# A layer's down-projection as seven half products instead of eight

## The reference, cut to what matters

```python
def conv_mlp(h, w_up, conv_w, w_down):
    u = dwconv3(h @ w_up, conv_w)
    gate, val = jnp.split(u, 2, axis=-1)
    return (jax.nn.silu(gate) * val) @ w_down      # (1024, 2816) @ (2816, 1024)

x = x + rmsnorm(y, norm_ffn_post)                  # y: the result of conv_mlp
h = rms_norm(x, l0_norm_2)                         # then the second block's first products
```

## Time and profile before

| | |
|---|---|
| Median of three runs | 1764.63 us (1763.34 to 1764.92) |
| Span of the profiled execution (the page gives no other time of it) | 1762.3 us |
| PE busy | 1737.1 us, 99% of the span |
| DVE, ACT, POOL busy | 1205.0, 787.1, 468.5 us |
| Down stage | 870.7 to 1111.4 us from the span's start |
| Mean granted TensorE clock | 0.999 |

### The profile page before, as it was taken

The page is one execution under the profiler, slowest core; times in us unless marked ns, Lnnn a source line. Parts: engine busy times, 40 slices in busy tenths (PEclk is TensorE's granted clock), DMA queues, the critical chain, the costliest instruction groups (busy, mean ns, idle before and its releaser), DMA issues.

```text
span 1762.3 us, 21154 instructions
## 1 busy us (share of the span) xinstructions
PE 1737.1 (99%) x8280; PEld 1424.6 (81%) x8280; DVE 1205.0 (68%) x1331; ACT 787.1 (45%) x1015; POOL 468.5 (27%) x201
## 2 busy tenths in 40 slices
PE   8999999999999999999999999999999999999998
PEld 5778888888787788888888888877888888888787
DVE  6454677859898887887764676755576767676534
ACT  5332222245335554544442443423366666666622
POOL 3357555364000000000164345122321211201151
PEclk9999999999999999999999999999999999999999
DMA  5233222145311222222464355412310111102232
GB/s 183 108 108 109 83 84 84 37 133 176 122 72 40 104 82 74 96 72 84 143 216 148 116 194 176 155 48 72 107 55 27 34 49 36 48 12 84 78 131 96
DMA packets 60588, 170.80 MB, mean 97 GB/s; under 512 B 7760, under 2 KB 10192, under 8 KB 60496
## 3 DMA queue, kind: packets, MB, share of 16 engines
q1 hardware_dynamic: 43216, 122.24, 20.9%
q10 hardware_dynamic: 17280, 47.30, 7.1%
HBM read 131.24 MB, written 38.27 MB: 96 GB/s over the span
## 4 chain that ended last, share of the span: by engine, by line
PE 89%; DVE 5%; ACT 3%; DMA 1%; issue 1%; ACTq 0%; SPq 0%; DVEq 0%
PE psum L732 21%; PE psum L1037 16%; PE psum L1050 14%; PE psum L771 5%; PE psum L1176 5%; PE psum L1201 5%; PE psum L927 5%; PE psum L1103 4%; PE psum L1210 4%; PE psum L1190 3%; DVE ptl L2492 2%; PE psum L753 1%; ACT pth L1824 1%; PE psum L1128 1%; PE psum L1310 1%
## 5 line engine op out<-in xcount | busy, mean ns | idle before, releaser
L643 POOL TENSOR_TENSOR wl<-wstage,wh 128x1024 fp32r<-128x1024 f32 x90 | 229.9, 2557 | 224.5 <-ACT wh L1337 192.2
L638 POOL TENSOR_TENSOR wh<-wstage,ones 128x1024 fp32r<-128x1024 f32 x43 | 103.0, 2396 | 463.3 <-PE psum L1176 298.8
L643 POOL TENSOR_TENSOR wx<-wstage,wx 128x1024 fp32r<-128x1024 f32 x25 | 61.5, 2462 | 493.6 <-ACT wx L1337 493.6
L732 PE MATMUL psum<-hh,wh 128*128 128x512 f32 x544 | 174.4, 402 | 0.0
L732 PE MATMUL psum<-hl,wh 128*128 128x512 f32 x544 | 168.0, 390 | 0.0
L732 PE MATMUL psum<-hh,wl 128*128 128x512 f32 x544 | 167.7, 389 | 0.0
L2213 DVE SCALAR_TENSOR_TENSOR cc<-uu,col,cc 128x1023 f32<-128x1023 f32 x88 | 114.9, 1306 | 44.6 <-ACT cc L1553 43.0
L732 PEld LDWEIGHTS psum<-hh,wh 128*128 128x128 f32 x544 | 100.2, 188 | 26.5 <-issue 5.6
L732 PEld LDWEIGHTS psum<-hh,wl 128*128 128x128 f32 x544 | 102.1, 188 | 21.9
L732 PEld LDWEIGHTS psum<-hl,wh 128*128 128x128 f32 x544 | 102.1, 188 | 21.6
L2492 DVE TENSOR_TENSOR ptl<-psum,pth 128x1024 fp32r<-128x1024 f32 x64 | 78.3, 1224 | 58.0 <-ACT pth L1824 58.0
(11 more groups left out here) (388 smaller groups left out, 4465.9 us busy)
## 6 DMA issues: line engine op xcount, KB each, us to landing
wstage<-w_units SPq DMA_DIRECT2D x161, 512.0 KB, 3.8
acts<-cc ACTq DMA_DIRECT2D x22, 512.0 KB, 2.6
hhf<-acts SPq DMA_DIRECT2D x27, 256.0 KB, 4.0
mix<-spill ACTq DMA_DIRECT2D x12, 512.0 KB, 2.6
resid<-yo SPq DMA_DIRECT2D x24, 256.0 KB, 2.2
hlf<-acts SPq DMA_DIRECT2D x17, 256.0 KB, 4.1
kq<-mix SPq DMA_DIRECT2D x16, 256.0 KB, 3.9
rstd<-gates ACTq DMA_DIRECT2D x16, 256.0 KB, 2.9
```

Of the source, the lines that this page charges most:

```text
L638: pool.tensor_tensor(high, stage(u), ones[:, :].unsqueeze(1).to_broadcast([P, 8, P]), ALU.mult).then_inc(w_high, 1)
L643: pool.tensor_tensor(low, stage(u), high.bitcast(F32), ALU.subtract).then_inc(w_split, 1)
L732: mm = pe.matmul(out[:, t], w[:, wslot, b, :], x[part][:, xk, t], start=start and n == 0, stop=stop and n == 2)
```

## The change

The stage is cut into blocks: the weights into W11, W21 (tiles 0 to 10, output tiles 0 to 3 and 4 to 7) and W12, W22 (tiles 11 to 21), the activations by tiles 0 to 10 and 11 to 21 and by T0 and T1. Instead of eight products of half size seven are made (f = 0 to 6), of `DK` = 11 steps each, with four output tiles a step: 12 matmuls a step, 77 steps. Several products need sums of weight blocks or of activation blocks as operands; DVE makes them in the stage (`left_sum`, `half_sums`), from blocks loaded half by half (`load_left`, `load_block`, `load_right`). POOL makes the low part of each weight half unit and the last product's activation difference. Two products that share a term share a PSUM bank: it is copied out by ACT (`taken`) and then goes on accumulating, and DVE adds the later ones to `yo` (`joined`).

| f | left (weights) | sum by DVE | right (activations) | sum | result to |
|---|---|---|---|---|---|
| 0 | W11 | none | tiles 0-10, T1 | none | m 0-3, T1 |
| 1 | W21 + W22 | yes | difference of T0 and T1 | DVE | m 4-7, T0 |
| 2 | f1's minus W11 | yes | tiles 11-21, T0 minus f1's | DVE | m 0-3, T0 |
| 3 | W12 minus f2's | yes | tiles 11-21, T0 | none | added, m 0-3, T0 |
| 4 | W11 minus W21 | yes | difference | DVE | added, m 4-7, T0; copied, T1 |
| 5 | W12 | none | tiles 11-21, T1 | none | added, m 0-3, T1 |
| 6 | W22 | none | difference | POOL | m 4-7, T1 |

The core of the diff:

```diff
+DK = FT // 2
+DOWNS = 7 * DK
 # PE
-            for half in range(2):
-                for k in range(FT):
-                    pe.wait_ge(w_split, U_DOWN + half * FT + k + 1)
-                    pe.wait_ge(a_lo, half * FT + k + 1)
...
+            def down(s):
+                f, p = divmod(s, DK)
+                high, low = left_place(s)
+                pe.wait_ge(w_split, U_DOWN + s + 1)
+                pe.wait_ge(a_lo, s + 1)
+                for m in range(4):
+                    if p == 0:
+                        down_free(f, m)
                     for n, (w, x) in enumerate(((high, ah), (high, al), (low, ah))):
...
+            for s in range(DOWNS):
+                down(s)
+                if s == 5 * DK + 3:
+                    pe.wait_ge(y_odd, 8)
+                    pe.wait_ge(y_even, 13)
+                    sum_half(0, KT - 1, 3)
 # places: weights in a ring of 4 half units, activations in one of 5
+            if U_DOWN <= u < U_L0:
+                return u - 3
 # SP
+            load_right(0)
+            load_right(1)
+            for s in range(DOWNS):
+                load_left(s)
+                if s + 2 < DK:
+                    load_right(s + 2)
+                if s < DK:
+                    load_block(s)
+                if 5 <= s < 5 + 2 * DK:
+                    load_right(DK + s - 5)
+                if 3 * DK + 5 <= s < 4 * DK + 5:
+                    load_block(DK + s - 3 * DK - 5)
+                if 4 * DK + 5 <= s < 5 * DK + 5:
+                    load_right(3 * DK + s - 4 * DK - 5)
 # POOL
+            def left_low(s):
+                pool.wait_ge(w_act, BY_ACT.index(U_DOWN + s) + 1)
+                high, low = left_place(s)
+                pool.tensor_tensor(low, left_source(s), high.bitcast(F32), ALU.subtract).then_inc(w_split, 1)
+            def last_right_sum(p):
+                pool.wait_ge(a_lo, 5 * DK + p + 1)
+                pool.tensor_tensor(right_z[p], right_z[p], right_x[p], ALU.subtract).then_inc(last_right, 1)
+            for s in range(DOWNS):
+                left_low(s)
+                if 5 * DK + 4 <= s < 6 * DK + 4:
+                    last_right_sum(s - 5 * DK - 4)
 # ACT
+            def down_parts(s):
+                right_half_high(s)
+                left_high(s)
+            def residual_moved(k):
+                residual_tile(2, 0, k, C_L0)
+                act.dma_start(resid2[k, :, T0], yo[:, k, T0]).then_inc(res_out, DMA)
+                if k + 2 < KT:
+                    act.dma_start(xr[:, k % 2, T0], resid1[k + 2, :, T0]).then_inc(xr_in[k % 2][0], DMA)
+            for s in range(7, DOWNS):
+                down_parts(s)
...
+                if s == 5 * DK + 6:
+                    half_roots(0, KT - 1, 3)
+                if 5 * DK + 7 <= s < 5 * DK + 7 + KT:
+                    residual_moved(s - 5 * DK - 7)
 # DVE
+            def half_sums(s):
+                f, p = divmod(s, DK)
+                if 1 <= f <= 4:
+                    left_sum(s)
+                if f in (1, 2):
+                    dve.wait_ge(*right_loaded(f * DK + p))
+                    dve.tensor_tensor(right_x[p], (right_z, right_w)[f - 1][p], right_x[p], ALU.subtract).then_inc(sw_sum, 1)
+                elif f == 4:
+                    dve.tensor_tensor(right_w[p], right_w[p], right_z[p], ALU.subtract).then_inc(sw_sum, 1)
+            def a_low(s):
+                half_sums(s + 2)
+                dve.wait_ge(a_hi, s + 1)
+                dve.tensor_tensor(al[s % DEEP], right_source(s), f32(ah[s % DEEP]), ALU.subtract).then_inc(a_lo, 1)
+            for s in range(7, DOWNS):
+                a_low(s)
...
+                if s == 5 * DK + 6:
+                    half_inverse(0, 3)
+                if 5 * DK + 7 <= s < 5 * DK + 7 + KT:
+                    residual_tile(2, 0, s - 5 * DK - 7, C_FPOST, C_L0)
```

More of the change, by code:

```diff
@@ L42 @@
 U_DOWN = U_SW + 7 * NS
-U_L0 = U_DOWN + 2 * FT
+DK = FT // 2
+DOWNS = 7 * DK
+U_L0 = U_DOWN + DOWNS
 U_ATT = U_L0 + 14
@@ L594, in _ @@
                 load_pair(q)
[L595 to L600, removed]
+            load_right(0)
[12 more added lines that the diff above has]
+                    load_right(3 * DK + s - 4 * DK - 5)
+            load(U_L0, loads(U_L0) % STG, U_L0 - 2)
+            for u in range(U_L0 + 1, U_L0 + 7):
                 load_unit(u)
@@ L1042, in _, with down_free @@
                 product(q, kind)
[L1044 to L1048, removed]
+            def down_free(f, m):
+                if f == 0:
+                    pe.wait_ge(up_evac, taken_after(FT - 1, "C11"))
+                elif f == 1:
+                    pe.wait_ge(val_taken, NS)
+                    pe.wait_ge(up_evac, taken_after(FT - 1, "C12"))
+                elif f < 5:
+                    pe.wait_ge(y_even, 4 * (f - 2) + m + 1)
+                else:
+                    pe.wait_ge(y_odd, 4 * (f - 5) + m + 1)
+                if (f, m) == (6, 3):
+                    pe.wait_ge(half_root, 3)
@@ L1699, in down_tiles @@
-            def down_tiles(half):
-                t = slice(half * HT, half * HT + HT)
[L1703 to L1721, removed]
@@ new lines, in squared @@
+            def squared(half, m):
+                t = slice(half * HT, half * HT + HT)
+                if m < 4:
+                    act.wait_ge(y_odd, 8 * half + m + 1)
+                elif not half:
+                    act.wait_ge(y_odd, m + 1)
+                else:
+                    act.wait_ge(*((y_odd, 13 + (m - 4) // 2) if m % 2 else (y_even, 14 + (m - 4) // 2)))
+                if m >= 3:
+                    act.wait_ge(acc_step, (KT - 1) * (2 + half) + m - 2)
+                act.activation(sq[:, m % 2, t] if m else root[:, t], yo[:, m, t], ACT.Square).then_inc(fsq_ready, 1)
@@ L2407, in _ @@
+            phase_done(6, 1)
+            dve.tensor_copy(yo[:, 5, T1], bank(down_bank(6, 1))).then_inc(y_odd, 1)
+            phase_done(6, 3)
+            dve.wait_ge(y_even, 13)
+            dve.tensor_tensor(yo[:, 7, T1], yo[:, 7, T1], bank(down_bank(6, 3)), ALU.add).then_inc(y_odd, 1)
+            for m in range(4, KT):
+                added(1, m)
             norm_inverse(2, 0)
```

330 lines of the change are left out of this document (210 added, 120 removed).

## The result

| | before | after |
|---|---|---|
| Median | 1763.99 us (1762.68 to 1764.92, 4 runs) | 1770.28 us (1769.25 to 1773.8, 4 runs) |
| Ratio to before | | 1.0041, 95% interval 1.0027 to 1.0055 |
| Span of the profiled execution | 1762.3 us | 1768.3 us |
| Down stage, first matmul to end of the last | 240.5 us | 249.3 us |

The change makes the kernel 0.4% slower (the two medians alone give 1.0036, inside the interval of the ratio). 132 matmuls are gone, and the stage lasts 8.8 us longer. The span grows only by 6.0: the stage starts 2.0 us earlier in this execution, though nothing ahead of it was changed, and what follows it is 0.7 us shorter.

What follows compares the result with a forecast made beforehand. PE was taken to bound the kernel, 99% busy, its residual loop hidden by the stage's lead. 1762.3 - 29.9 + 25.9 + 1.0 + 1.0 + 0.3 = 1760.6 us of span, plus 2.3: 1762.9, said as 1763; range 1759 to 1769.

Steps and rivals of the forecast that it cites:

- The removed matmuls: Down stage: 1056 matmuls become 924, so 132 x 0.2267 = 29.9 us of PE go, all on the path.
- The residual steps: Steps with residual tiles: loop through ACT and DVE stays 6.59 us; PE stands 25.9 us in steps 64 to 70.
- the transition: Start of the stage: four taps delay the first a_low; 0.3 us, between 0 and 3; f = 0 loads nothing, end 5.
- the prediction's own sign of being wrong: The prediction is wrong if, among other signs, PE stands at all in f = 0 for a DMA.
- the 445 GB/s of a third of a microsecond: Loads at the stage's start: rate of up to 445 GB/s brings a 256 KB block in 0.6 us.
- The clock: Rival, residual steps: clock falls in PE's gaps, only the last such step and the next late; 3 to 5 us, chance 0.05.
- a row with 8 matmuls evenly in 3 us: Profile row of before, cited against the clock falling: 3 us with 8 matmuls, where 13 would fit, were granted 1.00.
- The sums in f = 1, 2 and 4: DVE and POOL need 2.8 to 3.0 us a step; stall 1.0 us in f = 1 and 2, 1.0 in f = 4.
- the lead of 4.5 us: By step 9 DVE is 4.5 us ahead, set against 2 to 6 us lost over the 22 steps of f = 1, 2.
- The rival in which the port becomes the bound there: f = 1, 2 and 4: DVE and POOL need 3.3 us a step, 1775; chance 0.30 with all that ends slower.
- the far end of 1775: Whole kernel: upper of two far ends, 1752 to 1775, left out of the range of 1759 to 1769.
- the side to which I gave 0.30: Whole kernel: slower than the 1761.1 to 1768.2 us counted as the same, from the port and things unseen; chance 0.30.

Runs made afterwards that it cites:

- e2: Against the changed kernel, ScalarE takes each residual tile one down step later, behind the next step's rounding; 0.9988 of before, 1762.59 us, stage 239.7 us.
- e7: Changed kernel with block and activation loads issued later and GpSimd's f = 6 activation differences done on 2 of 512 columns; 0.9965 of before, 1757.73 us.
- e1: Against the changed kernel, only SyncE's load order changed: f = 1 block loads and f = 1, 2 activation loads issued later; 1.0004 of before, 1766.25 us.
- e9: Changed kernel with later loads, residual tiles one step later on ScalarE and spread, GpSimd's f = 6 differences placed where VectorE has room; 0.9942 of before, 1754.06 us.

## Why the prediction was wrong

**The removed matmuls** were right: 924 at 0.2267 us.

**The residual steps**, the large term, were right in mechanism and size: 6.49 us a step, forecast at 6.59; 26.4 us lost, forecast at 25.9. Only that all of it would be standing was not: PE stands 18.2 us and makes slow matmuls in the rest. The first GpSimd half held up the scaling and the second the low part, as followed through. e2 and e7 show both parts of it, the loop through ScalarE and the port.

**The step that failed is the transition**, where I wrote of f = 0 that it "asks for 39 such blocks in 30 us, 340 GB/s, most of them with six steps or more in hand: nothing taken, 5 us as the end". It took 8.1 us of stop and slow clock (0.3 were forecast), and e1 gets 7.5 of them back by the order of the loads alone. This is also the prediction's own sign of being wrong: PE stood in f = 0 for a DMA. One error was to take the 445 GB/s of a third of a microsecond for a rate that lasts. After shows 342 GB/s with the engines 98% busy; at that rate the 39 blocks of 256 KB need 30 us, and ScalarE's two stores of 512 KB come on top: there was no slack, and a block issued from 862 to 900 us was in its place 5.3 us later (median), not 0.6. The Trainium skill, DMA: Bandwidth & Descriptors, "Where 436 GB/s comes from", puts the limit of traffic from HBM at some 358 GB/s a core and that of the fabric at 435; the mean of 342 lies under the lower one, but six of those 27 us (874 to 880) ran at 389, so this trace does not show 358 as a ceiling. The other error was to see that SP's queue stands at `load_block(0)` and not to count what is left undone in the 6.8 us from one issue to the next: ScalarE stood 5.0 us for the weights of step 1 and could round them only at 868.0 us, and the queue entered f = 0 behind. How much of the 7.5 us belongs to the rate and how much to this stand stays open. That the first weight sum stands in VectorE's queue ahead of `a_low(9)` turned a late load for step 11 into a stop of step 9.

**The clock** was named as a rival with a chance of 0.05, at 3 to 5 us. Rows of after show granted clocks of 0.54 to 0.98 in the residual steps, a mixture of the two levels of 1.2 and 2.4 GHz, and 0.59 in step 9. Where nothing covered it, it cost 1.7 us (step 9, part of the 8.1) and 1.8 us (steps 70 to 76, for which the rival had 3 to 5; 0.2 in e1 and e7). The mechanism was right, also in that it costs nothing inside the loop; the chance was far too low, because I held a row with 8 matmuls evenly in 3 us against stops of 3 to 4 us.

**The sums in f = 1, 2 and 4** come out near, 2.7 us for 2.0, but by misses that nearly cancel. The step takes 2.91 us, where I had 2.8 to 3.0, and f = 1 and 2 lose 2.3 us for a forecast of 1.0; f = 4 loses nothing for another 1.0. The other 0.35 us are behind step 58, at the sum over partitions. Nor did the lead of 4.5 us last: in after 1.5 us of it cover steps 10 to 17, in e1 PE loses from step 8 on, where VectorE had stood 5.0 us for the first block. The rival in which the port becomes the bound there, with 3.3 us a step, did not occur.

In the stage the differences add up to 7.8 (f = 0) + 1.8 (clock behind step 70) + 0.7 + 0.5 = 10.8 us, which is 249.3 less the 238.5 that my terms give. The time came out only 7.3 us above mine, mostly because the stage starts 2.0 us earlier and what follows it is 0.7 shorter, in which nothing was changed: that is luck. At 1770.28 us it lies above my range of 1759 to 1769, short of the far end of 1775, on the side to which I gave 0.30: slower, and by the one term whose upper end I had set at 5 and carried into the sum as nothing.

What else stays open: e9 leaves 21.3 us between the stage and its matmuls, 4.1 of them in steps 10 to 58, 0.9 for the sum over partitions and 16.2 from step 59 on. DVE was busy for 217.0 us and POOL for 140.9 of its 230.8, both with their waits for the port, so a good part is that port; how much is still latency was not tried.

## What to carry to other kernels

Taking matmuls away shortens a step for every engine, not for PE alone: write down for each engine, port and queue what one step asks of it, and compare with the new length of the step; here a loop of 6.6 us that had been free at 5.4 us a step cost 26 us at 2.7. Rate a load burst by the GB/s of a stretch as long as the burst with the engines full, never by the best slice, and look how long the queue stands before the burst and who stands behind it. When work is moved off a full path, look first at which sum or reduction in PE's own stream passes through the place it is moved to.

## What the runs showed of the hardware that was not expected

- VectorE's and GpSimd's subtractions of 128x512, all inputs in SBUF: 0.60 and 1.29 us alone, 1.70 us a pair when they alternate, on both engines' rows.
- 256 KB loads issued from 862 to 900 us of after, with the DMA engines 98% busy from 868.8 on, landed 4.5 to 7.3 us after issue (medians by target); 4.0 to 4.1 us for the activation tiles in the stage of before, where the engines were 50% busy.
- PE with twelve matmuls in each 6.5 us and stops of 1.4 to 3.7 us between them gets a granted clock that differs from step to step (0.93, 0.54, 0.98, 0.76) though the steps are alike; with 24 instead of 12 matmuls in the same 6.5 us and stops of 0.4 to 1.1 us it stayed at 1.00.
